# A gated linear-algebra block on one core: the modulation product summed by VectorE, two thirds of its weight matrix read during later stages

## The reference, cut to what matters

```python
mod = jax.nn.silu(c) @ w_ada + b_ada          # c: 1x2048, w_ada: 2048x12288 float32
shift1, scale1, gate1, shift2, scale2, gate2 = jnp.split(mod, 6, axis=-1)   # 2048 each
h = rms_norm(x, norm1_w) * (1 + scale1) + shift1          # x: 256x2048
p = h @ w_in                                  # fourier part, q, k, v, output gate, 16 gates
mix = concat([fourier_mix(p), mlstm_bidirectional(p) * sigmoid(p)])
x = x + gate1 * (mix @ w_out)
h2 = rms_norm(x, norm2_w) * (1 + scale2) + shift2
u = depthwise_conv_centred(h2 @ w_up, w_conv, b_conv)
a, v = jnp.split(u, 2, axis=-1)
x = x + gate2 * ((silu(a) * v) @ w_down)
x = rms_norm(x, norm_f_w)
...
# a second block follows: a feed-forward, a mixer (state space, attention, merge), a feed-forward
```

## Time and profile before

| | before |
|---|---|
| median of three runs | 4088.96 us (4088.54 to 4096.41) |
| span of the profiled execution, first to last instruction | 4079.4 us |
| granted TensorE clock, mean over the span | 0.941 |
| PE busy | 3729.5 us, 91% |
| DVE busy | 2144.6 us, 53% |
| ACT busy | 1670.8 us, 41% |
| read from HBM | 690.93 MB |

### The profile page before, as it was taken

How to read it: one execution, slowest core, us unless ns; L and a number is a source line. 1 busy time by engine, 2 the same in 40 slices (tenths; PEclk the granted TensorE clock), 3 DMA queues, 4 the chain that set the end, 5 groups by cost and what they waited for, 6 DMA issues and landing times.

```text
span 4079.4 us, 60149 instructions
## 1 busy us (share of the span) xinstructions
PE 3729.5 (91%) x24246; PEld 3335.0 (82%) x24246; DVE 2144.6 (53%) x2328; ACT 1670.8 (41%) x1712; POOL 163.9 (4%) x257
## 2 busy tenths in 40 slices
PE   6879988999999979999998987846999979999998
PEld 3339757998899879989996985735999879989996
DVE  7983355565456554444445333499454454444444
ACT  7863334554344333333334322322333343333333
POOL 1000000000000000000000000055000000000000
PEclk9999989999999989999999996577999989999999
DMA  9986425665666656656664572000666556656664
GB/s 354 407 315 177 153 83 155 183 179 185 194 183 177 195 144 182 185 187 190 180 185 154 146 165 59 1 0 11 167 183 180 190 144 182 179 195 186 185 184 136
DMA packets 836208, 697.40 MB, mean 171 GB/s; under 512 B 11799, under 2 KB 761679, under 8 KB 834848
## 3 DMA queue, kind: packets, MB, share of 16 engines
q1 hardware_dynamic: 831184, 677.42, 55.3%
q0 software_dynamic: 4768, 18.84, 1.9%
q10 hardware_dynamic: 176, 0.07, 0.0%
HBM read 690.93 MB, written 5.36 MB: 171 GB/s over the span
## 4 chain that ended last, share of the span: by engine, by line
PE 81%; DVE 8%; DMA 5%; ACT 3%; issue 2%; POOL 1%; DVEq 0%; ACTq 0%; SPq 0%; POOLq 0%
PE ps L1710 17%; PE ps L1712 17%; PE ps L1711 17%; PE ps L1735 8%; PE ps L1736 8%; PE ps L1739 8%; DMA stage<-in_w_ada 4%; PE ps L2013 1%; DVE w_lo L1164 1%; PE ps L2090 1%; DVE w_lo L1031 1%; ACT w_hi L660 1%; PE ps L2034 1%; DMA stage<-in_w_in 1%; ACT w_hi L770 1%
## 5 line engine op out<-in xcount | busy, mean ns | idle before, releaser
L1031 DVE TENSOR_TENSOR w_lo<-stage,w_hi 128x2048 fp32r<-128x2048 f32 (+1 forms) x536 | 1211.1, 2261 | 1514.7 <-ACT w_hi L660 1514.5
L660 ACT ACTIVATE w_hi<-stage 128x2048 fp32r<-128x2048 f32 (+1 forms) x536 | 1012.2, 1889 | 1708.9 <-PE ps L1712 1115.3
L1710 PE MATMUL ps<-xt_hi,w_hi 128*128 128x256 f32 x5440 | 1550.6, 285 | 33.8 <-DVE w_lo L1031 25.1
L1711 PE MATMUL ps<-xt_lo,w_hi 128*128 128x256 f32 x5440 | 1547.0, 284 | 0.0
L1712 PE MATMUL ps<-xt_hi,w_lo 128*128 128x256 f32 x5440 | 1546.7, 284 | 0.0
L1710 PEld LDWEIGHTS ps<-xt_hi,w_hi 128*128 128x128 f32 x5440 | 1052.8, 194 | 37.5 <-DVE w_lo L1031 26.3
L1711 PEld LDWEIGHTS ps<-xt_lo,w_hi 128*128 128x128 f32 x5440 | 1052.8, 194 | 0.1
L1712 PEld LDWEIGHTS ps<-xt_hi,w_lo 128*128 128x128 f32 x5440 | 1052.2, 193 | 0.0
L1735 PE MATMUL ps<-w_hi,hid_hi 128*128 128x512 f32 x1184 | 461.8, 390 | 7.5 <-DVE w_lo L1031 7.5
L1736 PE MATMUL ps<-w_lo,hid_hi 128*128 128x512 f32 x1184 | 461.1, 389 | 0.0
L1739 PE MATMUL ps<-w_hi,hid_lo 128*128 128x512 f32 x1184 | 365.0, 389 | 0.0
(11 more groups left out here) (350 smaller groups left out, 3013.1 us busy)
## 6 DMA issues: line engine op xcount, KB each, us to landing
stage<-in_w_ada SPq DMA_DIRECT2D x96, 1024.0 KB, 6.5
stage<-in_w_in SPq DMA_DIRECT2D x92, 1024.0 KB, 5.6
stage<-in_w_up SPq DMA_DIRECT2D x88, 1024.0 KB, 5.6
stage<-in_ffn_w_gate SPq DMA_DIRECT2D x88, 1024.0 KB, 5.6
stage<-in_ffn_w_up SPq DMA_DIRECT2D x88, 1024.0 KB, 5.6
stage<-in_ffn_w_down SPq DMA_DIRECT2D x88, 1024.0 KB, 5.0
stage<-in_w_down SPq DMA_DIRECT2D x44, 1024.0 KB, 5.1
stage<-in_w_out SPq DMA_DIRECT2D x32, 1024.0 KB, 5.0
```

Of the source, the lines that this page charges most:

```text
L660: act.activation(w_hi[:, u % 2 * UNIT:u % 2 * UNIT + n], stage[:, u % SLOTS * UNIT:u % SLOTS * UNIT + n], ACT.Copy).then_inc(hi_made, 1)
L1031: dve.tensor_tensor(w_lo[:, part], stage[:, u % SLOTS * UNIT:u % SLOTS * UNIT + n], w_hi[:, part].bitcast(F32), ALU.subtract).then_inc(spl ...
L1710: pe.matmul(dst, wh, chunk(xh, k0 + k), start=start and k == 0, stop=False)
L1711: pe.matmul(dst, wh, chunk(xl, k0 + k), start=False, stop=False)
```

## The change

- `w_ada` is no longer split nor multiplied on PE. DVE multiplies a slice of 128 rows of `w_ada` by one column of silu(c) and adds it to an accumulator (`weigh`: the first slice by TENSOR_SCALAR, all others by SCALAR_TENSOR_TENSOR, 128x1024 each). When all 16 slices of a block of 2048 columns are in, PE sums over the partitions by 16 products with a column of ones (`fold`), DVE adds the bias (`take_mod`).
- Only shift1 and scale1 (32 units, whole rows of 8 KB per partition) come through `stage` ahead of `in_tiles`. The other four blocks come as 128 pieces of 512 KB (4 KB per partition), issued by POOL on its queue: 64 in `in_tiles` and `in_rows` (gate1, shift2; two pieces after each split, four buffers), 32 in the Fourier part, the heads and `out1` (scale2; two buffers), 32 in `up00` (gate2; one piece after each of 32 splits, four buffers). Each POOL load waits until its buffer's piece has been used.
- Accumulators of gate1, shift2 and scale2 lie in `x_nat`, so x is loaded again in `out1`, and `take_out1` waits for it. POOL loads x first of all now, and the Fourier matrices early.
- The round trip through memory (L419, L422, L1809) is gone; `take_mod` of a block waits for its fold.
- DVE's loop over `up00` is written out instead of looped. Several semaphores are shared (`f_dve`, `f_act`, `p_dve`, `p_act`) with the same order of waits.

```diff
-    mod_row = sb("mod_row", 6 * D, at=OV, parts=64)
+    acc1 = sb("acc1", 2 * D, at=OV)
+    late_ring = [sb("late0", HALF, at=FN + 8192), sb("late1", HALF, at=FN + 12288),
+                 sb("late2", HALF, at=RB), sb("late3", HALF, at=RB + 4096)]
+    late_pair = [sb(f"late_x{k}", HALF, at=XN + 8192 + 4096 * k) for k in range(2)]
+    late_gate = [sb(f"late_f{k}", HALF, at=FN + 4096 * k) for k in range(4)]
+    late_acc = [sb("acc_g1", D, at=XN), sb("acc_s2", D, at=XN + 8192), sb("acc_c2", D, at=XN),
+                sb("acc_g2", D, at=RB)]
...
-                    if u >= SLOTS or not fresh:
-
-                        step = 2 if name == "ada" else 1
-                        sp.wait_ge(used, before + (i * body_units + u - SLOTS + 1) * step)
+                    if name == "ada":
+                        if u >= SLOTS or not fresh:
+                            sp.wait_ge(S["ada_acc"], 2 * (i * body_units + u - SLOTS + 1))
+                    elif name == "in_tiles" and fresh:
+                        sp.wait_ge(S["ada_acc"], 2 * (ADA - SLOTS + u + 1))
+                    elif u >= SLOTS or not fresh:
+                        sp.wait_ge(used, before + (i * body_units + u - SLOTS + 1))
...
+        ada = I["w_ada"].rearrange("(k p) n -> k p n", p=P)
+        load("ada", 16, 2, lambda i, u: [(slot(u % SLOTS), ada[u][:, i * D:(i + 1) * D])])
...
+        pool.dma_start(x_nat[:, :].rearrange("p (m d) -> p m d", m=MT),
+                       I["x"].rearrange("b (m p) d -> p (b m) d", p=P)).then_inc(S["x_in"], 16)
...
+        def late_source(n):
+
+            at = 2 * D + n // 32 * D + n % 2 * HALF
+            return ada[n % 32 // 2][:, at:at + HALF]
+
+        for n in (2, 3, 0, 1, *range(4, 64)):
+            if n >= 4:
+                pool.wait_ge(S["late_acc"], n - 3)
+            elif n < 2:
+                pool.wait_ge(S["norm_turned"], 8)
+            pool.dma_start(late_ring[n % 4][:, :], late_source(n)).then_inc(late_in[n % 4], 16)
+
+        pool.wait_ge(S["mod_made"], 3)
...
+        pool.wait_ge(S["late_acc"], 64)
         pool.dma_start(mask1[:, :].rearrange("p (k n) -> p k n", n=T), I["k_mask"]).then_inc(S["mask_in"], 16)
         spread_row(I["mlstm_norm_w"], D - 1024)
+        pool.wait_ge(S["mod_turned"], 4)
+        for n in range(64, 96):
+            if n >= 66:
+                pool.wait_ge(S["late_acc"], n - 1)
+            pool.dma_start(late_pair[n % 2][:, :], late_source(n)).then_inc(late_in[n % 2], 16)
+        pool.wait_ge(S["late_acc"], 96)
+        pool.wait_ge(S["mod_turned"], 5)
+        pool.dma_start(x_nat[:, :].rearrange("p (m d) -> p m d", m=MT),
+                       I["x"].rearrange("b (m p) d -> p (b m) d", p=P)).then_inc(S["x_in"], 16)
         spread_row(gates_dram[0])
+        pool.wait_ge(S["norm_turned"], 16)
+        for n in range(96, 128):
+            if n >= 100:
+                pool.wait_ge(S["late_acc"], n - 3)
+            pool.dma_start(late_gate[n % 4][:, :], late_source(n)).then_inc(late_in[n % 4], 16)
+        pool.wait_ge(S["mod_made"], 6)
+        pool.dma_start(gates_dram[1].rearrange("(k p) -> p k", p=P), mod[:, 80:96]).then_inc(S["gate_out"], 16)
+        pool.wait_ge(S["gate_out"], 32)
...
+                def split_up(i, u):
+                    split(name, 4, i, u)
+                    if gating and 4 <= 4 * i + u < 36:
+                        late(92 + 4 * i + u, 1)
+
+                def pending():
+                    take(0, 1)
+                    if n == 0:
+                        take_mod(5, bank(7, 0, 16))
...
-        def ada(i):
-            for h in range(32):
-                dve.wait_ge(hi_made, 32 * i + (h + 1))
-                at = slice(h % 4 * HALF, (h % 4 + 1) * HALF)
-                dve.tensor_tensor(w_lo[:, at], stage[:, h % 8 * HALF:(h % 8 + 1) * HALF],
-                                  w_hi[:, at].bitcast(F32), ALU.subtract).then_inc(split_made, 1)
-        ada(0)
+        def weigh(dst, src, k):
+
+            if k == 0:
+                return dve.tensor_scalar(dst, src, csilu[:, 0:1], None, ALU.mult)
+            return dve.scalar_tensor_tensor(out=dst, in0=src, scalar=csilu[:, k:k + 1], in1=dst,
+                                            op0=ALU.mult, op1=ALU.add)
+
+        def ada(u):
+            dve.wait_ge(landed[u % SLOTS], 16 * (u // SLOTS + 1))
+            for h in range(2):
+                n = 2 * u + h
+                if u % KC:
+                    dve.wait_ge(S["ada_acc"], n - 1)
+                weigh(acc1[:, u // KC * D + h * HALF:u // KC * D + (h + 1) * HALF],
+                      stage[:, u % SLOTS * UNIT + h * HALF:u % SLOTS * UNIT + (h + 1) * HALF],
+                      u % KC).then_inc(S["ada_acc"], 1)
+
+        def late(first, count):
+
+            for n in range(first, first + count):
+                k, h = n % 32 // 2, n % 2
+                if n < 64:
+                    src = late_ring[n % 4]
+                    dve.wait_ge(late_in[n % 4], 16 * (n // 4 + 1))
+                elif n < 96:
+                    src = late_pair[n % 2]
+                    dve.wait_ge(late_in[n % 2], 16 * (16 + (n - 64) // 2 + 1))
+                else:
+                    src = late_gate[n % 4]
+                    dve.wait_ge(late_in[n % 4], 16 * ((32 if n % 4 < 2 else 16) + (n - 96) // 4 + 1))
+                if k:
+                    dve.wait_ge(S["late_acc"], n - 1)
+                elif n < 32:
+                    dve.wait_ge(S["norm_xhat"], 2)
+                elif 64 <= n < 96:
+                    dve.wait_ge(S["mod_turned"], 3)
+                weigh(late_acc[n // 32][:, h * HALF:(h + 1) * HALF], src[:, :], k).then_inc(S["late_acc"], 1)
...
+        def take_mod(b, src):
+
+            dve.wait_ge(S["mod_turned"], b + 1)
+            dve.tensor_tensor(mod[:, 16 * b:16 * b + 16], src, cols[:, C_ADA + 16 * b:C_ADA + 16 * b + 16],
+                              ALU.add).then_inc(S["mod_made"], 1)
...
+        dve.wait_ge(S["csilu_made"], 1)
+        for u in range(KC):
+            ada(u)
         norm_scale(0)
-        with dve.Fori(1, 6) as i:
-            ada(i)
...
+        for u in range(KC + 8, ADA):
+            ada(u)
+        split("in_tiles", 4, 0, 0)
+        dve.wait_ge(S["mod_turned"], 2)
...
+            take_mod(b, bank(7, 16 * b, 16))
+        scale_of(0)
         norm_finish(0, scale_cols[:, 0:KC], mod[:, 0:16])
-        for u in range(1, 4):
-            split("in_tiles", 4, 0, u)
-        with dve.Fori(1, 4) as i:
-            for u in range(4):
-                split("in_tiles", 4, i, u)
+        late(0, 2)
+        for t in range(1, 16):
+            split("in_tiles", 4, t // 4, t % 4)
+            late(2 * t, 2)
         dve.memset(v_one[:, :].rearrange("p (k n) -> p k n", n=257)[:, :, 256:257], 1.0)
         for u in range(16):
             split("in_rows", 16, 0, u)
+            late(32 + 2 * u, 2)
+            if u == 2:
+                take_mod(2, bank(7, 0, 16))
+        take_mod(3, bank(1, 0, 16))
...
             rest(xt_lo[:, at], turn[:, g % 2 * 512:(g % 2 + 1) * 512], xt_hi[:, at], S["mix_lo"])
+            late(64 + 4 * g, 4)
...
             last.then_inc(S["num_taken"], 1)
+            late(80 + h, 1)
...
             rest(xt_lo[:, at], turn[:, g % 2 * 512:(g % 2 + 1) * 512], xt_hi[:, at], S["mix_lo"])
+            late(84 + 2 * g, 2)
...
         for u in range(4, 16):
             split("out1", 16, 0, u)
+            if u in (4, 5):
+                late(92 + 2 * (u - 4), 2)
+            if u == 7:
+                take_mod(4, bank(7, 0, 16))
+                scale_of(1)
             if u == 9:
+                dve.wait_ge(S["x_in"], 32)
                 take_out1(0)
...
                     pe.wait_ge(S["rows_taken"], 2 * rows_index[f"down{n}0"] + 1)
+                    if n == 0:
+                        pe.wait_ge(S["late_acc"], 128)
+                        fold(late_acc[3][:, :], 7, 0)
...
-        pe.wait_ge(S["crep_made"], 1)
...
-        with pe.Fori(0, 6) as i:
...
-                        pe.matmul(dst, a, w_hi[:, at + n * 512:at + (n + 1) * 512], start=k == 0, stop=False)
-                        last = pe.matmul(dst, a, w_lo[:, at + n * 512:at + (n + 1) * 512], start=False,
-                                         stop=k == KC - 1)
-                    last.then_inc(split_used, 1)
...
-        pe.wait_ge(S["ada_taken"], 14)
         norm(0, range(4))
-        pe.wait_ge(S["modrow_in"], 32)
-        for v, t in enumerate((conv_a, conv_v)):
-            last = pe.matmul(bank(7, 0, 96), t[0:96, 0:P], ident[0:96, 0:96], start=v == 0, stop=v == 1)
-        last.then_inc(S["mod_turned"], 1)
-        pe.wait_ge(S["mod_made"], 1)
-        norm(0, range(4, 8))
+        pe.wait_ge(S["cols_made"], 1)
+        norm(0, range(4, 7))
+
+        def fold(acc, b, at):
+
+            for j in range(KC):
+                last = pe.matmul(bank(b, at + j, 1), acc[:, j * P:(j + 1) * P], ones_col[:, :], start=True, stop=True)
+            last.then_inc(S["mod_turned"], 1)
```

(23 more changed lines are left out.)

168 lines of the change are left out of this document (63 added, 105 removed).

## The result

The changed kernel takes **3965.32 us** (median of 4 runs, 3964.2 to 3968.85) against 4088.75 us before (4 runs, 4085.19 to 4096.41): a ratio of 0.9696, 95% interval 0.9682 to 0.971, so 3.0% faster. I had forecast 3955 within 3936 to 3988, faster with a chance of 0.96. The profiled execution's span is 3962.1 us against 4079.4.

A forecast was written before the change was run, and what follows sets the result against it. Transfers were taken to bound the `w_ada` units, PE `in_tiles` and `in_rows`. Costs of 47.8 us against -182 gave -134: span 3945 from 4079.4, and 3955 for the median run, 9.6 above the span; range 3936 to 3988.

The forecast's parts named there:

- The main term: First stage, up to `in_tiles`' first product: fewer bytes to land bring that product at 108.6 instead of 290.9, -182 us.
- The rule of about 358 GB/s: Path from HBM: first stage 107 us instead of 98, estimate 3972, not used in the sum; chance 0.03.
- Term 2: `in_tiles` and `in_rows`: two pieces after each split hidden; +1.3 second split, +1 transfers, +3.4 fold behind `in_rows`.
- Term 3: Fourier loop: DVE waits for two buffers to be refilled, 5.1 us per pair of pieces; +17.8 us.
- Term 4: Heads: one piece after each of four costs +3.6 us, a longer wait before the first head +3.
- Term 5: `out1`: pieces through two buffers +8.9 us, lower-clock restart +1.8, fold +2.5, second load of x +1; together +14.2.
- Term 6: `up00`: pieces hidden in the gaps, +1 us; fold of gate2 before `up01`, +2.5.
- Transfers as the bound of `in_tiles` and `in_rows`: Rival: two rings need 6.8 and 5.9 us per unit there; 23 us more, 3978; chance 0.14.
- Slower landing at 6 us: Rival: POOL's pieces land in 6 us, not 3.8, lengthening ten waits in Fourier loop and `out1`; 3977; chance 0.12.
- DVE not fitting its gaps: Rival: next unit's split waits for both pieces after ACT's copy; 35 us if missed by a microsecond, 3990; chance 0.03.
- POOL's loads at 12 us: Rival: each POOL load takes 12.1 us like x, cancelling the net gain; 4101 at 13 us; chance 0.03.

The follow-up runs named there:

- the experiment on the order: Changed kernel with POOL loading the Fourier matrices behind the 64 pieces and the two early pieces after the first norm; span 3953.7 us against 3962.1.
- four buffers: Changed kernel with scale2's pieces through four buffers in the Fourier loop and three behind it, instead of two; 3946.59 us, ratio 0.9649 to the kernel before.
- DVE's work alone: Changed kernel without 30 of scale2's 32 loads, DVE's 32 products kept on two loaded pieces; span 3948.0 us, Fourier loop 28.4 us.
- runs without loads: Changed kernel without 60 of the 64 piece loads of `in_tiles` and `in_rows`, DVE's products kept; span 3960.4 us against 3962.1.

## Why the prediction was right, and which of its terms were not

**The main term** was right in mechanism and size: -180.4 for -182. The first stage is bound by transfers (393 and 410 GB/s in the windows of after; 5.2 us for 2.1 MB in the experiment on the order). The 1.6 us missing are the fold in front of `take_mod`, which I had hidden under the split: its products take twice the time of the later folds', 6.99 us, and DVE waits 2.02 for it.

**The rule of about 358 GB/s.** The prediction weighed this rate for a core's path from HBM, of the Trainium skill (SBUF — State Buffer, section "A bandwidth-pool intuition that's wrong (but worth ruling out)"). The changed kernel's first stage moved 393 and 410 GB/s, so the trace disagrees here too. The Trainium skill (Perfetto Trace Analysis, section "Roofline") has that rate as the share of a core when both of a pair draw on the memory and lets one core alone have more; the trace agrees.

**Term 2**, +10.0 for +5.7. The steps on the pieces were right: they fit the gaps by 1.07 and 0.76 us where I had 1.1 and 0.7, and the transfers cost nothing that the runs can show (204.5 us for the stretch without 60 of the loads, 204.8 with all of them in the experiment on the order). The two pieces ahead of the second split cost less than the 1.3 that I gave them: all of `in_tiles` grew by 0.6. The step that failed is the price of a fold, and it failed in the reading of a row. I took the earlier trace rows for 60 products, 0.155 us each. They are 60 records of 30 products (the loops around L1922 make 2 times 15), two records each as in the fold, so the row says 0.31 us a product. And that is a mean over two clocks, as the windows of the kernel before show:

```profile
2318.70:2322.00 3.30, 3.30 (x31) 3.27 (x30) 1.96 (x1) 1.58 (x2) 0.00 (x0) 1.00 0.98 267
2322.90:2328.00 5.10, 5.10 (x26) 5.10 (x26) 0.00 (x0) 0.00 (x0) 0.00 (x0) 0.50 0.77 206
```

31 records in 3.3 us are 0.21 us a product at the full clock, and 26 in 5.1 are 0.39 at the lower one. The fold's products take 0.22: 3.5 us for 16, not 2.5. The same rows held the other thing that I missed: less than 4 us into these narrow products, without a gap of PE, the granted clock fell, and it was still 0.50 in the 3.5 us behind them. I put the clock behind a fold at nothing, with no reason given. And I said that the fold before `in_rows` is hidden under ACT's last copies: PE goes from `in_tiles` to `in_rows` in 4.9 us with it, and did in 2.9 before.

**Term 3**, +22.6 for +17.8. Mechanism right, as four buffers and DVE's work alone show (both 28.4 us): 16.1 us of the loop are waits for two buffers, 6.5 DVE's products. The pair's period was mis-sized: 5.1 forecast, 5.7 measured. In the expectation for four buffers I put the difference on POOL's issue of 0.53 us. The timeline of POOL says otherwise:

```profile
360.54 0.53 POOL L466 DMA_DIRECT2D late_x<-in_w_ada  x1 [2.92 <-DVE acc_c L1180]
363.03 0.53 POOL L466 DMA_DIRECT2D late_x<-in_w_ada  x1 [1.96 <-DVE acc_c L1180]
365.93 0.53 POOL L466 DMA_DIRECT2D late_x<-in_w_ada  x1 [2.37 <-DVE acc_c L1180]
```

The piece begun at 361.45 ends at 362.73, POOL starts the issue at 363.03, and DVE begins that buffer's next piece at 366.84: 1.28 + 0.30 + 3.81 = 5.4, and the landing counts from the issue's start, so its 0.53 are in the 3.81. The other pairs are longer by landings of up to 4.7. So the 0.6 us are many small ones: 0.2 of lag, 0.1 of use, 0.1 to 0.5 of landing.

**Term 4**, +5.6 for +6.6, right: 4.4 from `ecols` to `out1`'s first product, 1.3 in `out1`'s first units. That the 1.3 is PE's restart at the lower clock isn't tested by itself.

**Term 5**, +17.9 for +14.2. Unit 4's first product came 26.3 us behind the first copy where it was 15.0: +11.2 for my 8.9 + 1.8. From there to `take_out1(0)` it is 32.9 us for 26.3, 6.6 more: again the fold, 3.5 for 2.5, and the clock behind it and behind the waits (granted 0.84 from 481 to 492 us).

**Term 6**, +7.0 for +3.5: from `norm_scale(1)`'s product to the last product of `down00` it is 425.1 us, and was 425.2, so the pieces in `up00` cost nothing; the fold before `up01` cost 6.6 where I had 2.5. The 0.5 that are left lie in the part that varies by more than that from one execution to the next.

**What lies around the span.** I took the 9.6 us between before's profiled span and its median run for a constant outside the instructions. It is not: the changed kernel's profiled run took 3964.2 us for a span of 3962.1, and one of the later runs of before 4083.58 for 4081.8. So 2 us lie outside, and before's profiled execution was simply some 7.5 us faster than its median. On spans my sum was 16.9 us too low; this second error, of the other sign, left 10.3 of it in the forecast of the time. That is luck: with 2 us in place of 9.6 the forecast would have been 3947. A span should be compared with a span.

**The rivals.** Transfers as the bound of `in_tiles` and `in_rows`: splits at their old period, so no. Slower landing at 6 us: a median of 3.9 in the two-buffer stretches, though 3.8 to 6.4 in `out1`. DVE not fitting its gaps: no. POOL's loads at 12 us: no, though beside SP's loads they take 7.0. None took place. The measured 3965.3 lies inside the range, and even inside the forecast's own spread of 3938 to 3970, but with the right distance between span and time that spread would have ended at about 3962: the range held because it was widened for rivals that did not come, and what came instead, the price of folds and pairs, about 17 us, was less than the 22 and 23 that they asked for. One of their prices is off: POOL's loads at 13 us would also lengthen the units of `in_tiles` and `in_rows`, by another 14 us, which makes about 4115 and not 4101.

## What to carry to other kernels

Work moved off a saturated resource is free only where another engine bounds: the same 1.2 us piece cost nothing behind a split under PE's units and all of itself, plus a refill wait, in a chain DVE, ACT, PE. Before a transfer is put under such work, count its buffers: a piece's period is its landing, the lag of the issue and its use, divided by the number of buffers, and it must lie below the work's own. And when a profile is the base of a sum, ask first whether its span is a typical one.

## What the runs showed of the hardware

- Behind a fold of one-column products the granted clock was low although PE had no idle gap: 0.52 in the 6 us behind the fold before `up01`. It was so behind 22 of the 24 narrow folds that follow the first stage in the six traces that have four of them whole; behind scale2's fold in the runs without loads and on the order it stayed at 1.00, and why isn't known. The fold before `up01` cost 5.1 to 6.7 us in these traces. With 128 columns per product, the same 32 weight loads and the same 3.5 us, the clock stayed at 1.00 behind all 11 folds that PE's work followed within 0.6 us, and the seam cost 3.6. The Trainium skill (TensorE: Matmul & The Clock Gate, section "HAM oscillation — how this bites in real kernels") tells of falls after idle gaps; by that alone a fold would cost its 3.5 us and nothing behind, and the trace does not bear that out.
- A 128x128 product in f32 with one moving column leaves two records and takes 0.22 us at the full clock, as long as with 128 columns. One with a stationary operand of 33 rows and 16 moving columns takes 0.21 (31 records in 3.3 us in the kernel before).
- A 512 KB load from POOL's queue lands in 3.9 us (median) where it is nearly alone, in 7.0 beside SP's 1 MB loads and pieces of its own kind, counted from the start of POOL's issue.
- What stays open: why the unchanged part from `norm_scale(1)` on varied by 6 us between executions, most of it in the second block, and why PE's restarts in `out1` stayed at the lower clock longer in some runs than in others.
